# Stick-breaking heads with stationary probabilities and outputs with queries on partitions

## The reference

```python
def stick_breaking_attention(q, k, v, g):
    for start in range(0, S, Q_BLOCK):            # 128 queries
        end = start + Q_BLOCK
        qb, kb, vb = q[:, start:end], k[:, :end], v[:, :end]
        z = jnp.einsum('bqhd,bkhd->bhqk', qb, kb).astype(jnp.float32) * scale
        mask = jnp.arange(end)[None, :] < (start + jnp.arange(Q_BLOCK))[:, None]
        log_1mb = jnp.where(mask, jax.nn.log_sigmoid(-z), 0.0)
        suffix = lax.cumsum(log_1mb, axis=3, reverse=True) - log_1mb
        a = jnp.where(mask, jnp.exp(jax.nn.log_sigmoid(z) + suffix), 0.0)
        outs.append(jnp.einsum('bhqk,bkhd->bqhd', a.astype(vb.dtype), vb))
    o = jnp.concatenate(outs, axis=1)
    return rmsnorm(o, g).reshape(B_, S, SB_WIDTH)
```

## Time and profile before

| | us |
|---|---|
| median of 3 runs | 3777.23 |
| lowest, highest | 3773.42, 3777.32 |
| the profiled run, its own time | 3776.57 |
| its span in the profile | 3774.2 |

### The profile page before, as it was taken

How to read it: one execution, slowest core, us unless ns; L and a number is a source line. 1 busy time by engine, 2 the same in 40 slices (tenths; PEclk the granted TensorE clock), 3 DMA queues, 4 the chain that set the end, 5 groups by cost and what they waited for, 6 DMA issues and landing times.

```text
span 3774.2 us, 58634 instructions
## 1 busy us (share of the span) xinstructions
PE 3707.6 (98%) x24136; PEld 3087.4 (82%) x24136; DVE 1829.6 (48%) x3365; ACT 1381.0 (37%) x2503; POOL 462.8 (12%) x237
## 2 busy tenths in 40 slices
PE   8999999999999999999999999999999999999999
PEld 6888788978897888976887779888777888887887
DVE  5657625451644455557655665554654222232223
ACT  4332421321232454565656655545552200020001
POOL 2001130000000000233233330000001000000000
PEclk9999999999999999999999999999999999999999
DMA  8756686557655877866666656545325655464554
GB/s 309 273 185 229 236 290 245 209 202 251 218 193 194 279 254 245 272 208 223 228 224 219 207 197 225 169 148 180 130 104 187 229 189 190 181 236 175 184 199 158
DMA packets 198874, 799.34 MB, mean 212 GB/s; under 512 B 20816, under 2 KB 70224, under 8 KB 130384
## 3 DMA queue, kind: packets, MB, share of 16 engines
q1 hardware_dynamic: 198608, 795.59, 60.7%
HBM read 594.18 MB, written 201.33 MB: 211 GB/s over the span
## 4 chain that ended last, share of the span: by engine, by line
PE 92%; DVE 4%; ACT 2%; issue 1%; DMA 1%; SPq 0%; DVEq 0%; ACTq 0%
PE bank L1402 87%; PE bank L1406 4%; DVE P L2484 1%; DVE P L2486 1%; DVE R L2145 0%; ACT P L1940 0%; ACT P L1939 0%; DVE Z1a L2192 0%; DVE Qb L2235 0%; SPq L2688 0%; DVE Tb L2236 0%; DMA slot<-Wd 0%; ACT L1939 0%; DMA KS<-Kd 0%; DVE Kb L2237 0%
## 5 line engine op out<-in xcount | busy, mean ns | idle before, releaser
L1402 PE MATMUL bank<-Z1a,slot 128*128 128x512 f32 x3048 | 786.1, 402 | 9.4 <-DVE slot L2083 9.4
L1402 PE MATMUL bank<-Z1b,slot 128*128 128x512 f32 x3048 | 780.9, 401 | 4.5 <-DVE Z1b L2192 4.4
L1402 PE MATMUL bank<-slot,Z0b 128*128 128x512 f32 (+1 forms) x3504 | 708.9, 353 | 7.2 <-DVE AF L2214 5.3
L1402 PEld LDWEIGHTS bank<-Z1a,slot 128*128 128x128 f32 x3048 | 568.0, 190 | 141.2 <-DVE slot L2083 9.4
L1402 PEld LDWEIGHTS bank<-Z1b,slot 128*128 128x128 f32 x3048 | 565.5, 189 | 139.1 <-issue 6.8
L1402 PEld LDWEIGHTS bank<-slot,Z0b 128*128 128x128 f32 x3504 | 563.0, 189 | 99.8 <-DVE AF L2214 6.0
L2648 POOL TENSOR_TENSOR slot<-raw,slot 128x1024 fp32r<-128x1024 f32 x110 | 289.9, 2643 | 645.5 <-ACT slot L1823 645.4
L2145 DVE SCALAR_TENSOR_TENSOR R<-bank,small,R 128x512 f32<-128x512 f32 x352 | 261.1, 749 | 208.2 <-PE bank L1402 207.7
L1402 PE MATMUL bank<-KS,DQ 128*128 128x512 f32 (+3 forms) x960 | 281.4, 389 | 9.3 <-DMA KS<-Kd 4.8
L2452 DVE TENSOR_SCALAR_CACHE_REDUCE P<-bank 128x512 f32<-128x512 f32 (+3 forms) x320 | 189.2, 608 | 199.0 <-PE bank L1402 198.4
L2660 POOL TENSOR_TENSOR Z0b<-AF,Z0b 128x512 fp32r<-128x512 f32 x88 | 126.6, 1439 | 1235.2 <-ACT Z0b L2013 1235.2
(11 more groups left out here) (235 smaller groups left out, 4551.2 us busy)
## 6 DMA issues: line engine op xcount, KB each, us to landing
slot<-Wd SPq DMA_DIRECT2D x390, 1024.0 KB, 4.9
Wd<-slot SPq DMA_DIRECT2D x130, 1024.0 KB, 6.8
raw<-in_wts_dram SPq DMA_DIRECT2D x130, 512.0 KB, 4.2
DQ<-Qd SPq DMA_DIRECT2D x192, 128.0 KB, 3.7
DV<-Vd SPq DMA_DIRECT2D x60, 256.0 KB, 4.5
KS<-Kd SPq DMA_DIRECT2D x24, 512.0 KB, 7.5
KS<-Kd SPq DMA_DIRECT2D x24, 384.0 KB, 6.9
zraw<-Yd SPq DMA_DIRECT2D x16, 512.0 KB, 5.5
```

The source lines that it names most:

```text
L1402: return e.matmul(o, a, b, start=start, stop=stop, skip_group_check=True)
```

## The change

For stick heads `TP` becomes the stationary operand and the 64 columns of `DV` the moving one, all blocks of keys accumulate in one region of bank 6 of 128 queries by 64 features, and the output is squared with the accumulator read and copied on ScalarE like a differential unit's. The two halves stand side by side in `OR`. The finish is the differential heads', with eight factors for each query instead of four, without the factor's VectorE part, and with `sb_g` as scale in `fd b`. `BO`, its three memsets, VectorE's addition and the stages `fs a`, `fs b`, `fs c` are gone. In the planner `o` costs ScalarE 540 for all units. `at_ss` and `at_fac` get 2 x `NT` columns.

```diff
-            if e < 4:
-                P.put(("o", u), ("act", 540), after=P.clock["pe"] + 200)
-            else:
-                P.put(("o", u), ("act", 280), ("dve", 280), after=P.clock["pe"] + 200)
+            P.put(("o", u), ("act", 540), after=P.clock["pe"] + 200)
             if last:
-                P.add(self.finish_diff(i, s, e) if e < 4 else self.finish_stick(i, s, e), slack=SLACK_C)
+                P.add(self.finish(i, s, e), slack=SLACK_C)
...
-    def finish_stick(self, i, s, e):
-        P = self.P
-        t = P.put(("fs a", i), ("act", 610))
-        yield t
-        yield P.end[self.tp_uses[-2]]
-        self.tp_uses.append(("fs b", i))
-        t = P.put(("fs b", i), ("pe", 900), ("act", 2000), after=t)
-        for c in range(NT):
-            yield t
-            t = P.put(("fs c", i, c), ("dve", 1500), after=t)
...
                     if e_ < 4:
                         x = mm(bank[6][:, 0:128], tp[:, tok(k)], DV[:, t, :], t == 0, t == nb - 1)
                     else:
-                        h = t % 2
-                        x = mm(bank[6][64 * h:64 * h + 64, 0:128], DV[:, t, 64 * half:64 * half + 64], tp[:, tok(k)],
-                               t < 2, t >= nb - 2)
+                        x = mm(bank[6][:, 0:64], tp[:, tok(k)], DV[:, t, 64 * half:64 * half + 64], t == 0, t == nb - 1)
...
-            def finish_stick(i):
-                if (free := tp_free(("fs b", i))) is not None:
-                    pe.wait_ge(*free)
-                pe.wait_ge(*act_fin("fs a", i))
-                pe.wait_ge(*dve_c("one1"))
-                mm(bank[4 + tp_no["fs b", i] % 2][:, :], BO[:, :], PY[:, :], True, True).then_inc(*pe_tr.inc("fs b", i))
...
+                w = 128 if e_ < 4 else 64
+                k = qt if e_ < 4 else 2 * qt + half
+                e.activation(PY2[:, 0:w], bank[6][:, 0:w], ACT.Square, accum_out=at_ss[i % 3][:, k:k + 1])
+                e.activation(OR[i % 2][:, qt, w * half:w * half + w], bank[6][:, 0:w], ACT.Copy).then_inc(*act_o.inc("o", u))
...
+                elif kind == "fd a":
+                    act.wait_ge(*act_o("o", UNITS.index((s, e_, 1, NT - 1))))
+                    if i >= 3:
+                        act.wait_ge(*dve_fin("fd a", i - 3, "o"))
+                    e.activation(at_fac[i % 3], at_ss[i % 3], ACT.Sqrt, scale=1.0 / 64, bias=rms_eps).then_inc(
+                        *act_fin.inc("fd a", i))
...
-            def outputs(u):
-                s, e_, half, qt = UNITS[u]
-                if ("o", u) in dve_o.at:
-                    dst = OR[HEADS.index((s, e_)) % 2][64 * half:64 * half + 64, qt, :]
-                    dve.wait_ge(*act_o("o", u))
-                    e.tensor_tensor(dst, bank[6][0:64, 0:128], dst, ALU.add).then_inc(*dve_o.inc("o", u))
...
+            def finish(i):
+                diff = HEADS[i][1] < 4
+                dve.wait_ge(*act_o("o", UNITS.index((*HEADS[i], 0 if diff else 1, NT - 1))))
+                if diff:
+                    finish_factor(i)
+                fac = at_fac[i % 3][:, 0:NT if diff else 2 * NT]
+                dve.wait_ge(*act_fin("fd a", i))
+                e.reciprocal(fac, fac).then_inc(*dve_fin.inc("fd a", i, "r"))
+                dve.wait_ge(*dve_fin("fd a", i, "r"))
+                w = 128 if diff else 64
+                rows_ = OR[i % 2][:, :, :].rearrange("p c (h n) -> p (c h) n", n=w)
+                e.tensor_tensor(rows_, rows_, bc(fac, w, 2), ALU.mult).then_inc(*dve_fin.inc("fd a", i, "o"))
...
-            def finish_stick(i, c):
-                t = tok(c)
-                dve.wait_ge(*act_fin("fs b", i))
-                e.reciprocal(PY[:, t], PY[:, t]).then_inc(*dve_fin.inc("fs c", i, c, "r"))
-                dve.wait_ge(*dve_fin("fs c", i, c, "r"))
-                e.scalar_tensor_tensor(PY[:, t], OR[i % 2][:, c, :], pcol("sb_g"), PY[:, t], ALU.mult, ALU.mult).then_inc(
-                    *dve_fin.inc("fs c", i, c, "y"))
```

More of the change, by code:

```diff
@@ L1142, in build @@
         act_o = signal("act_out", of("o"))
-        act_fin = signal("act_finish", [st for st in order if st[0] in ("fd a", "fd b", "fs a", "fs b")])
+        act_fin = signal("act_finish", [st for st in order if st[0] in ("fd a", "fd b")])
         act_n2 = signal("act_norm2", of("n2"))
@@ L1684, in tensor @@
                 elif kind == "fd b":
-                    finish_diff(*a)
-                elif kind == "fs b":
-                    finish_stick(*a)
+                    finish(*a)
                 elif kind == "rb":
```

85 lines of the change are left out of this document (21 added, 64 removed).

## The result

The changed kernel takes **3788.1 us** (median of 8 runs, 3783.1 to 3791.8) against 3775.9 for the kernel before (8 runs, 3773.0 to 3778.0). The ratio is 1.0032, with an interval from 1.0021 to 1.0043. The forecast was 3775.6 us and "within .2%"; the change is 12 us slower.

A forecast was written before the change was run, and what follows sets the result against it. TensorE, busy 98% of the span, was taken as the bound. Value runs +8, finish -3.6, VectorE's relief -8, ScalarE +1 and a new wait +1 gave -1.6 us, forecast 3775.6 us, range 3761 to 3790.

The forecast's parts named there:

- new pass: Stick value matmuls on TensorE: 64 moving columns against 128 stationary ones still take .11 us a pass, the upper bound.
- premise that a load can't start before the present weights are in use: TensorE's value matmuls: weight loading therefore sets the pace, keeping a pass of 64 moving columns at .11 us.
- full run: A stick value run of four blocks on TensorE, entry and exit included: .79 us becomes .90, +.10 us (.06 to .15).
- all stick runs: TensorE's 147 stick value runs together: sum +7.1 us, 3 to 12, taken as +8.
- The finish: Head's end on TensorE: eight times four transposes (.45 us) replace a matmul with `BO` (.90 us), -3.6 us.
- projection matmuls before a run: Sign in the later profile: six projection matmuls in front of a stick value run are back at 1.39 us.
- VectorE's finish of `OR`: New wait: reciprocal and product wait for ScalarE's square root, delaying VectorE's queue and TensorE; +1 us, from 0 to 18.
- VectorE's relief: Without additions in front of scans, TensorE waits less for VectorE's product and `AF`: -8 us (0 to -20).
- second rival: Most TensorE waits caused by VectorE and its successors vanish, some 20 of 29 us: 3763 us, chance 21%.
- ScalarE was to grow by 10 to 30 us: Stick outputs add a square and accumulator read to ScalarE's copy; mostly covered, +1 us of time, 0 to 4.
- waits of over 8 us at places that I haven't read: Failure sign: the prediction fails if the changed order makes waits of this size at unread places.
- third rival: VectorE's finish waits for the square root, ScalarE's longer output delays `TP`, eating the relief: +10, 3787 us, chance 20%.

The follow-up runs named there:

- old-order run: The changed kernel's instructions, with output and finish planned at the old costs and stages so each engine keeps the earlier kernel's order: 3765.3 us, ratio .9968.

## Why the prediction was wrong

**What held.** The new pass comes at the pace of the differential one, as the loads said (192 ns; the run with 128 moving columns shows it). The premise that a load can't start before the present weights are in use fits the rows before: in the differential runs no load starts earlier than 1 ns after the start of the matmul before it. The full run costs +.106 us with its ends, and all stick runs in the old order together +7.0 us where +8 was taken. (The text of the old-order run has 8.4, which the traces don't bear out.) The finish wasn't measured alone; at four of its eight places TensorE is .41 to .46 us shorter, where .45 was taken, and at the others the neighbours or the clock changed too. The projection matmuls before a run are back at 1.40. No VectorE row waits for an `OR` copy in front of a scan, and TensorE's waits for VectorE's product are .5 us. TensorE still waits once, 3.1 us, for VectorE's finish of `OR`, as it did before the change (both have it at a differential head), and no other wait for that finish shows. What it delayed on VectorE behind it wasn't measured alone.

**What was mis-sized.** VectorE's relief was put at -8 us. The run without the additions measured **-14**. I counted 1.6 us for each of five product waits and three for one `AF`; all of the product waits went, and most of `AF`. This is the second rival's mechanism ("relief goes further"), though not its 20 us, and in the old order its time, 3763, would have come near: +7 - 3.6 - 14 = -11, as measured. ScalarE was to grow by 10 to 30 us and stayed level, because the three operations of a stick output overlap (.43 us in all against .27 for the copy before) and eight times the head's square of 128x512 (632 ns) and root (687) are gone for a copy (682) and a small root (299). That makes +10 - 3; why the other 7 are missing too wasn't traced. ScalarE's total bore on nothing.

**The step that failed** is none of the terms of the sum. It is the assumption under it, that the rest of the program stands as it stood, for which the sum has no term at all and the text no reason but three places that were compared. The prediction named it as a sign of being wrong, "waits of over 8 us at places that I haven't read", and the sign came true. The change alters what the planner is told of the output and the finish, and some 870 of the 3111 runs of equal matmuls in TensorE's order have no match in the old order. That order costs 23 us, with the new instructions or the old. Of these, 16.6 are in the table of waits: 5.4 for the late `DV` load, 4.1 for `PT`, 1.7 for `QS`, 2.9 for `Z1b` (3.5 less .6), 3.4 for `R` (4.7 less 1.3) and smaller ones, against which the old order has 3.1 for a `TP` and 2.4 before a value run of its own. Some 5 more are the granted clock (.9952 to .9939), for which the sum has no term either. Against the kernel before, the measured +12.2 us are +2.7 of waits, some +5 of clock and the rest, 4 to 5, TensorE's own work. The forecast of -1.6 had -6 for the waits (-8 + 1 + 1), nothing for the clock and +4.4 for the work. So the work was right, and the waits and the clock account for the miss.

**The third rival** had nearly the right time (3787), by luck: neither the waits for the finish nor the delayed `TP` that it was made of are in the trace. The range (3761 to 3790) held the time, by width and not by reason.

**What would have warned me.** Line by line, the order of the changed program was there to read. The pooling matmul stood right behind a transposition where projection work used to stand, and the `DV` load stood behind a raw load. Whether the cover in TensorE's order had shrunk at the waits for `Z1b`, `QS` and `R` too wasn't looked up. I looked at the order only where my terms lay, at the value runs and the additions.

## What to carry to other kernels

Where a planner sets the order, split such a change in two, the new instructions in the old order and the old instructions in the new order: here the first gained 11 us, beating both kernels, and the second lost 23. Count a wait of TensorE with what its clock does afterwards: 5.4 us here cost over 7. Before an order is taken for neutral, compare, wherever TensorE's next instruction depends on several VectorE operations or on a load, how much independent work stands in front of it before and after. And an operation of .28 us that waits for another engine costs what is queued behind it: sixty of them cost the kernel 14 us, on an engine that was busy half of the time.

## What was not expected of the hardware

- Within a run, a float32 pass of 64 moving columns against 128 stationary ones comes at the pace of one of 128, every .112 us. The shorter form saved .05 us only where a run of eight had a transposition behind it.
- More than half of the column-tiled form's lead was lost at its ends. Eight passes took .588 us against .835 in the full form, and .106 us of that lead was left with the neighbours counted in, though each of its loads was recorded at 137 ns against 192.
- Two executions of one program, with sums of waits .5 us apart, were 5.6 us apart (3781.4 and 3787.0), at a granted clock of .996 and .993.
- ScalarE's square, its read of the accumulator and the copy behind it overlap. Their recorded durations add up to some 700 ns, but from the first start to the last end pass .43 us with 64 columns and .53 with 128:

```profile
1708.58 0.24 ACT L1939 ACTIVATE PY<-bank 128x64 f32<-128x64 f32 x1
1708.68 0.23 ACT L1939 ACTIVATION_READ_ACCUMULATOR PY<-bank 128x1 f32 x1
1708.77 0.25 ACT L1940 ACTIVATE OR<-bank 128x64 f32<-128x64 f32 x1
```
